# One down unit earlier, first transfers reordered, an idle bank and a scalar-engine transpose in a two-block transformer kernel

## The reference

```python
# first block, per layer: 8 + 2 heads, an index branch, a convolution branch, a recurrence, a gated FFN
xn = rms_norm(h, norm_mix[l]); proj = xn @ w_in[l]            # 1024 x 7464
y_a = dsa_attention(rope(q), rope(k), v, rope(qi), rope(ki), wi)   # top-64 keys of each query by an index score
y_b = sc_b * causal_dwconv(sc_c * sc_u, w_conv)
y_c = rwkv7_time_mix(rw_z, ...)   # state = state*w + (state @ ka)*kb + v*k over 256 steps, 8 heads
up = einsum('bsgc,gcd->bsgd', [y_a, y_b, y_c], w_branch[l])
h = h + sum(sigmoid(gate_pre + b_gate) * up) @ w_out[l]
h = h + (silu(conv(x @ w_up)[gate]) * conv(x @ w_up)[up]) @ w_down      # d_ff = 2816
# second block, per layer
u = rms_norm_2(x, norm_w) @ w_in                               # 1024 x 10240
ya = dilated_mixture(rope(qa), rope(ka), va) * silu(za)
ob = diff_attention(..., lam)     # lam = exp(lq1.lk1) - exp(lq2.lk2) + lambda_init
x = x + (sigmoid(ga) * (ya @ w_proj_a) + sigmoid(gb) * (yb @ w_proj_b)) @ w_out
```

## Time and profile before

| | us |
|---|---|
| median of 3 runs (lowest, highest) | 1663.52 (1663.13, 1664.37) |
| the profiled execution: its own time | 1662.3 |
| the profiled execution: its span | 1660.5 |
| PE busy | 1639.6 (99%) |
| DVE busy | 1186.5 (71%) |
| ACT busy | 970.8 (58%) |
| POOL busy | 191.3 (12%) |
| mean granted TensorE clock | 0.997 of full speed |

### The profile page before, as it was taken

The page is one execution under the profiler, slowest core; times in us unless marked ns, Lnnn a source line. Parts: engine busy times, 40 slices in busy tenths (PEclk is TensorE's granted clock), DMA queues, the critical chain, the costliest instruction groups (busy, mean ns, idle before and its releaser), DMA issues.

```text
span 1660.5 us, 27388 instructions
## 1 busy us (share of the span) xinstructions
PE 1639.6 (99%) x11188; PEld 1418.6 (85%) x11188; DVE 1186.5 (71%) x1666; ACT 970.8 (58%) x1484; POOL 191.3 (12%) x197
## 2 busy tenths in 40 slices
PE   8999999999999999999999999999999999999998
PEld 6999999988888999998988877778888887787886
DVE  6877456699888976547798885767756657667655
ACT  6674525565567565345655565665774546657743
POOL 0673500000001845200000000000000000000000
PEclk9999999999999999999999999999999999999999
DMA  7543532555555534425455555345345464344452
GB/s 268 174 153 109 178 116 103 180 177 202 179 194 182 173 106 140 160 103 178 152 200 199 178 186 194 131 149 174 130 162 188 170 204 151 130 175 144 141 197 76
DMA packets 48621, 270.11 MB, mean 163 GB/s; under 512 B 13617, under 2 KB 14513, under 8 KB 16753
## 3 DMA queue, kind: packets, MB, share of 16 engines
q1 hardware_dynamic: 38304, 265.22, 46.1%
q10 hardware_dynamic: 9424, 2.10, 0.6%
q0 software_dynamic: 768, 1.05, 0.2%
HBM read 266.51 MB, written 1.84 MB: 162 GB/s over the span
## 4 chain that ended last, share of the span: by engine, by line
PE 87%; DVE 7%; ACT 3%; issue 1%; DMA 1%; DVEq 0%; SPq 0%; ACTq 0%
PE bank L2769 10%; PE bank L2771 10%; PE bank L2770 10%; PE bank L1569 8%; PE bank L1570 7%; PE bank L1571 7%; PE bank L1627 7%; PE bank L1629 3%; PE bank L1730 3%; PE bank L1732 3%; PE bank L1731 3%; DVE w_low L1017 3%; DVE arena L1202 2%; PE bank L2799 2%; ACT w_high L605 1%
## 5 line engine op out<-in xcount | busy, mean ns | idle before, releaser
L1017 DVE TENSOR_TENSOR w_low<-slab,w_high 128x2048 fp32r<-128x2048 f32 x249 | 574.3, 2316 | 206.8 <-ACT w_high L605 199.7
L605 ACT ACTIVATE w_high<-slab 128x2048 fp32r<-128x2048 f32 x249 | 470.5, 1897 | 118.2 <-PE bank L2771 70.0
L1569 PE MATMUL bank<-act,w_high 128*128 128x256 f32 (+1 forms) x1136 | 328.7, 289 | 1.5 <-DVE w_low L1017 1.0
L1570 PE MATMUL bank<-act,w_high 128*128 128x256 f32 (+1 forms) x1136 | 321.2, 283 | 0.0
L1571 PE MATMUL bank<-act,w_low 128*128 128x256 f32 (+1 forms) x1136 | 321.1, 283 | 0.0
L2769 PE MATMUL bank<-w_high,act 128*128 128x512 f32 x768 | 305.6, 398 | 0.8 <-DVE act L2536 0.6
L2771 PE MATMUL bank<-w_low,act 128*128 128x512 f32 x768 | 299.8, 390 | 0.0
L2770 PE MATMUL bank<-w_high,act 128*128 128x512 f32 x768 | 299.0, 389 | 0.0
L1569 PEld LDWEIGHTS bank<-act,w_high 128*128 128x128 f32 (+1 forms) x1136 | 216.3, 190 | 10.8 <-issue 5.6
L1570 PEld LDWEIGHTS bank<-act,w_high 128*128 128x128 f32 (+1 forms) x1136 | 216.5, 191 | 0.7 <-issue 0.5
L1571 PEld LDWEIGHTS bank<-act,w_low 128*128 128x128 f32 (+1 forms) x1136 | 216.4, 190 | 0.0
(11 more groups left out here) (272 smaller groups left out, 2131.6 us busy)
## 6 DMA issues: line engine op xcount, KB each, us to landing
slab<-stream_a SPq DMA_DIRECT2D x143, 1024.0 KB, 4.9
slab<-stream_b SPq DMA_DIRECT2D x104, 1024.0 KB, 4.9
arena<-x_t SPq DMA_DIRECT2D x4, 256.0 KB, 6.7
slab<-stream_a ACTq DMA_DIRECT2D x2, 512.0 KB, 6.1
residual<-x_tok SPq DMA_DIRECT2D x1, 1024.0 KB, 10.9
lora_weights<-lora SPq DMA_DIRECT2D x2, 512.0 KB, 9.2
lora_weights<-final_rows SPq DMA_DIRECT2D x2, 512.0 KB, 5.8
d_inverse<-arena POOLq DMA_DIRECT2D x2, 256.0 KB, 2.4
```

The source lines that it names most:

```text
L605: line.did(eng.activation(core.wh[u % PARTS][:, 0:SLAB_WIDTH[u]], core.slab[u % SLABS][:, 0:SLAB_WIDTH[u]], ACT.Copy), core.sem("slab_high"))
L1017: line.did(line.eng.tensor_tensor(core.wl[u % PARTS][:, 0:SLAB_WIDTH[u]], core.slab[u % SLABS][:, 0:SLAB_WIDTH[u]], core.wh[u % PARTS][:, ...
L1569: eng.matmul(out, wh, xh, start=first, stop=False, skip_group_check=True)
L1570: eng.matmul(out, wh, xl, start=False, stop=False, skip_group_check=True)
```

## The change

Down unit i stands behind up unit 2i+4 instead of 2i+5 (except the last three, which stay at the end). The first transfers go x, slab 1, slab 2, tokens, 128 KB of the constants, slab 3; `vec_a`, the rest of the constants, slab 4, `const_a`, `lora` and slab 5 follow. The sines are computed ahead of everything else on ACT, with their table as the first one loaded; the root table is loaded before slab 1 is rounded, and squares, norm and rotary tables of stage a0 come behind unit `w0`. `post(1)` uses bank 5 instead of 7. POOL no longer makes the transposed copy nor writes to DRAM: ACT does both (`flip`, ahead of `gb0`), and the sixteen read-backs are shared, eight by ACT (ahead of `gb2`), eight by POOL. The split of the last quarter of the mixture stands behind the split of the next slab (`mix_low`). In the second block the product behind `lam` is made at the start of a stage, `norm` stands behind `v` unit 0, and the two extra squares of b0 behind its transposes. Semaphores that are merged (`rates_made`, `lora_inputs`, `model_in`) keep their meaning; those hunks, the table of counts and the hunks that only pass new names are left out here.

```diff
@@ -47,18 +47,15 @@
            + [("out", i) for i in range(4)])
-LAG_DOWN = 2
 NARROW_UP = 4
 def ffn_units():
-    units = []
-    for pair in range(FT // 2 + LAG_DOWN):
-        if pair < FT // 2:
-            units += [("up", 2 * pair), ("up", 2 * pair + 1)]
-        if pair >= LAG_DOWN:
-            units.append(("down", pair - LAG_DOWN))
-    return units
+    downs = FT // 2
+    units = [("up", j) for j in range(3)]
+    for i in range(downs - 3):
+        units += [("up", 2 * i + 3), ("up", 2 * i + 4), ("down", i)]
+    return units + [("up", FT - 3), ("up", FT - 2), ("up", FT - 1)] + [("down", i) for i in range(downs - 3, downs)]
 UNITS_A += ffn_units()
@@ -241,6 +238,7 @@
 GEMM_BANKS = 3
+ATTENDED = (6, 5)
 def plan(units):
@@ -358,11 +356,10 @@
     if first:
-        steps = [("angles", 0)]
+        steps = [("angles", 0), ("angles", 1)]
         for n in range(2):
             steps += [("scaled", n), ("round_half", n), ("split_half", n)]
-        return (steps + [("scaled", 2), ("scaled", 3), ("round", 1), ("split", 1), ("angles", 1), ("root_table", 0),
-                         ("square", 0), ("square", 1), ("angles", 2), ("norm", 0)])
+        return steps + [("scaled", 2), ("scaled", 3), ("root_table", 0), ("round", 1), ("split", 1)]
     return [("add", 0), ("add", 1), ("add", 2), ("scaled", 0), ("scaled", 1), ("add", 3), ("square", 0), ("square", 1), ("split", 1)]
@@ -421,6 +418,8 @@
         amid(("w", 0), ("x_turn", 2), ("x_turn", 3))
+    if first:
+        put(("w", 0), ("square", 0), ("square", 1), ("norm", 0), ("angles", 2))
     amid(("w", 1), *([] if first else [("norm", 0)]), ("tables", 0))
@@ -447,8 +446,9 @@
     put(("ga", 3), ("tok", 2))
+    amid(("gb", 0), ("flip", 0))
     put(("gb", 0), ("off_diag", 0), ("bonus_shift", 0))
-    put(("gb", 2), ("blocks_in", 0))
+    amid(("gb", 2), ("blocks_in", 0))
     put(("gb", 3), ("solve", 0))
@@ -460,6 +460,7 @@
     amid(("br2", 1), ("mix", 0))
+    put(("br2", 1), ("mix_low", 0))
     amid(("out", 2), ("x_ffn", 0), ("x_ffn", 1))
@@ -490,8 +491,10 @@
                 put(UNITS_B[host + n], ("turn_late", 8 * kind))
-    mid = {("v", 0): [("x_turn", 2), ("x_turn", 3)], ("v", 1): [("norm", 0)]}
+    mid = {("v", 0): [("x_turn", 2), ("x_turn", 3)]}
+    put(("v", 0), ("norm", 0))
     if first:
+        mid["v", 0] += [("square", 2), ("square", 3)]
         mid["out", 3] = [("x_next", 0), ("x_next", 1)]
@@ -510,9 +513,7 @@
     put(("out", 2), ("root_table", 0))
-    lead = lead_steps(False)
-    if first:
-        lead[lead.index(("split", 1)):] = [("square", 2), ("square", 3), ("split", 1)]
+    lead = [("lam_product", 0)] + lead_steps(False)
     return woven(UNITS_B, False, lead, after, mid, not first, behind_mid=[("v", 0)])
@@ -550,22 +551,25 @@
     slab_to(core, eng, 1)
+    slab_to(core, eng, 2)
     eng.dma_start(core.h[:], d["x_tok"]).then_inc(sem("tokens_in").sem, 16)
-    eng.dma_start(core.cc[:], d["common"]).then_inc(sem("const_in").sem, 16)
-    slab_to(core, eng, 2)
-    eng.dma_start(core.cm[:], d["const_a"]).then_inc(sem("model_in").sem, 16)
-    eng.dma_start(core.vec[:], d["vec_a"][0]).then_inc(sem("vec_in").sem, 16)
-    eng.dma_start(core.lora[:], d["lora"][0]).then_inc(sem("lora_in").sem, 16)
+    eng.dma_start(core.cc[:, 0:2 * P], d["common"][:, 0:2 * P]).then_inc(sem("const_in").sem, 16)
     for u in range(SLABS, SLABS_IN_ALL):
...
         slab_to(core, eng, u)
+        if u == SLABS:
+            eng.dma_start(core.vec[:], d["vec_a"][0]).then_inc(sem("vec_in").sem, 16)
+            eng.dma_start(core.cc[:, 2 * P:], d["common"][:, 2 * P:]).then_inc(sem("model_in").sem, 16)
+        if u == SLABS + 1:
+            eng.dma_start(core.cm[:], d["const_a"]).then_inc(sem("model_in").sem, 16)
+            eng.dma_start(core.lora[:], d["lora"][0]).then_inc(sem("lora_in").sem, 16)
         if u == FIRST_SLAB["a1"] + SLABS:
...
         if u == FIRST_SLAB["b0"] - 20:
-            eng.dma_start(core.cb[:], d["const_b"]).then_inc(sem("const_b_in").sem, 16)
+            eng.dma_start(core.cb[:], d["const_b"]).then_inc(sem("model_in").sem, 16)
             eng.wait_ge(sem("g_made").sem, START["b0"]["g_made"])
@@ -655,6 +659,18 @@
              core.sem("rooted_sums"))
+def inverses_from(core, eng, by, blocks):
+    eng.wait_ge(*core.sem("inverses_written").next(eng, 16))
+    for at, turned, name in ((TD_, 1, "transposes_in"), (UD_, 0, "inverses_in")):
+        to = flat(core, at, 4).rearrange("p (cj t) -> p cj t", cj=16)
+        for n in blocks:
+            q = n % 4
+            eng.dma_start(to[SUB * n:SUB * n + SUB, :, SUB * q:SUB * q + SUB],
+                          core.d_inverse[SUB * n:SUB * n + SUB, turned, :].rearrange("cj (i t) -> i cj t", i=SUB)
+                          ).then_inc(core.sem(f"{name}_{by}").sem, 16)
 WIDTH = {0: P, 1: T}
@@ -863,7 +879,7 @@
         eng.wait_ge(*sem("outputs_turned").next(eng))
-        act(core.xh[:, 2 * n:2 * n + 2, :], heads(bank[6 + n], T), ACT.Copy, sem("ya_high"))
+        act(core.xh[:, 2 * n:2 * n + 2, :], heads(bank[ATTENDED[n]], T), ACT.Copy, sem("ya_high"))
     def lora_inputs(_):
@@ -929,15 +945,18 @@
                 sem("blocks_written").sem, 16)
+    def flip(_):
+        both = flat(core, UT_, 2)
+        eng.wait_ge(*sem("inverted").next(eng))
+        ut = both.rearrange("p (w i t) -> p w i t", w=2, i=SUB)
+        act(ut[:, 1], ut[:, 0].rearrange("p i t -> p t i"), ACT.Copy)
+        line.settled()
+        eng.dma_start(core.d_inverse, both.rearrange("p (w n) -> p w n", w=2)).then_inc(sem("inverses_written").sem, 16)
     def blocks_in(_):
-        eng.wait_ge(*sem("inverses_written").next(eng, 16))
-        to = flat(core, UD_, 4).rearrange("p (cj t) -> p cj t", cj=16)
-        for n in range(8):
-            q = n % 4
-            eng.dma_start(to[SUB * n:SUB * n + SUB, :, SUB * q:SUB * q + SUB],
-                          core.d_inverse[SUB * n:SUB * n + SUB, 0, :].rearrange("cj (i t) -> i cj t", i=SUB)
-                          ).then_inc(sem("inverses_in").sem, 16)
+        inverses_from(core, eng, "act", range(4, 8))
     def solve(s):
@@ -986,7 +1006,7 @@
     eng.wait_ge(*sem("eps_set").next(eng))
-    line.did(eng.activation(core.small[:, 6:7], core.small[:, 0:1], ACT.Copy))
+    line.did(eng.activation(core.small[:, 6:7], core.small[:, 0:1], ACT.Sin))
     eng.wait_ge(sem("gains_in").sem, 16)
@@ -1258,7 +1278,7 @@
                     did(tt(flat(core, GA_ + at, 2), flat(core, GA_ + at, 2), src, ALU.add), sem("summed"))
-                if g == 2 and (i or k):
+                if g == 2 and i + k == 1:
                     for at_ in ((0, 2) if i == 0 else (at,)):
@@ -1271,6 +1291,9 @@
             ffn(i)
+    def mix_low(_):
+        low(14, 2, core.a(GA_ + 6, 2), "mix_high", "mix_ready")
     def ki_turn(_):
@@ -2011,7 +2037,7 @@
             eng.wait_ge(sem("dve_emptied7").sem, banks.count[7, "dve"])
-        b = 6 + n
+        b = ATTENDED[n]
         banks.fill(b, "dve")
@@ -2290,13 +2318,7 @@
     def blocks_in(_):
-        eng.wait_ge(*sem("inverses_written").next(eng, 16))
-        to = flat(core, TD_, 4).rearrange("p (cj t) -> p cj t", cj=16)
-        for n in range(8):
-            q = n % 4
-            eng.dma_start(to[SUB * n:SUB * n + SUB, :, SUB * q:SUB * q + SUB],
-                          core.d_inverse[SUB * n:SUB * n + SUB, 1, :].rearrange("cj (i t) -> i cj t", i=SUB)
-                          ).then_inc(sem("transposes_in").sem, 16)
+        inverses_from(core, eng, "pool", range(4))
     def blocks_turn(_):
@@ -2321,11 +2343,7 @@
             did(tt(above, above, term, ALU.add))
-        line.settled()
-        did(eng.tensor_copy(ut[:, 1], u.rearrange("p i t -> p t i")))
-        line.settled()
-        eng.dma_start(core.d_inverse, flat(core, UT_, 2).rearrange("p (w n) -> p w n", w=2)).then_inc(
-            sem("inverses_written").sem, 16)
+        line.tell(sem("inverted"))
     def off_diag(_):
@@ -2554,17 +2573,18 @@
         if stage == "b0":
-            eng.wait_ge(sem("const_b_in").sem, 16)
+            eng.wait_ge(sem("model_in").sem, 48)
         line.settled()
...
         line.settled()
-    def lam(_):
+    def lam_product(_):
         q = core.gains[:, GN["lam"] + 4 * layer:][:, 0:4].rearrange("p (n two) -> p n two", two=2)
         did(tt(core.small[:, 14:16].unsqueeze(2), q[:, :, 0:1], q[:, :, 1:2], ALU.mult), sem("lam_products"))
+    def lam(_):
         eng.wait_ge(*sem("act_emptied6").upto(1))
```

More of the change, by code:

```diff
@@ L874, in lora @@
             for b in range(2):
-                eng.wait_ge(*sem(("decay_made", "rate_made")[half]).next(eng))
+                eng.wait_ge(*sem("rates_made").upto(2 * b + half + 1))
                 for k in range(2):
@@ L978, in scalar_a @@
                                scores=scores, turn=turn, post=post, lora_inputs=lora_inputs, lora=lora, decay=decay, blend=blend,
-                               kk_square=kk_square, kk_root=kk_root, tok=tok, blocks_out=blocks_out, blocks_in=blocks_in, solve=solve,
```

(11 more changed lines are left out.)

37 lines of the change are left out of this document (21 added, 16 removed).

## The result

The changed kernel takes **1652.80 us** (median of 6 runs, 1652.70 to 1653.18), the one before 1663.14 on the same chip (6 runs, 1661.46 to 1664.37): ratio 0.9937, 95% interval 0.9927 to 0.9947. The forecast was 1653.5, with a range of 1649.5 to 1658.0. The profiled execution took 1652.78 with a span of 1651.0: 9.5 us less than before, where the sum said 9.9. By the medians the gain is 10.3: the kernel before spreads over 2.9 us and the changed one over 0.5. In the runs of the kernel before that stand beside the experiments, those with a mean granted clock of 0.999 or 1.0 took 1661.15 to 1662.98 and those with 0.997 took 1662.65 to 1664.50; every run of the changed kernel had 0.999 or 1.0.

What follows compares the result with a forecast made beforehand. PE, busy 1639.6 of 1660.5 us, was taken as the bound, leaving idle time and half-clock stretches to win. Terms of 9.9 us off 1662.3 gave 1652.4; 1.2 for the median made 1653.5, range 1649.5 to 1658.0.

Steps and rivals of the forecast that it cites:

- the sum: All six parts together: 3.6 + 2.4 + 0 + 1.0 + 1.0 + 1.9 = 9.9 us gained.
- Part 1: Start: slab 3 rounded earlier, q0 at full clock, a new wait at `turns`; gain 3.6 us, bounds 2.5 and 6.
- The table load: ACT at the start: a load costs 1.28 us without the skill's 1.38 drain, which would cut the gain by about 1.4.
- Part 2: Bank 5 for `post(1)`: PE's two waits for ACT's copy out of bank 7 go, 2.4 us in the sum.
- Part 3: Inverses shared between ACT and POOL: worth 0 us, bounds -1 and +1, as it protects the gain of bank 5.
- PE shows no wait at the solve steps now: Solve steps: no wait listed now, and none expected after the bank and inverse changes, hence 0 us.
- Its side: ACT's `flip`: at 179.3 less the start's gain; slab `gb3` keeps some 6 us to spare, so PE doesn't see it.
- Rival D: ACT stands in `flip`, delaying the rounding for `gb3` past its 6 us to spare: slower, 1667.6 us; chance 0.03.
- Part 4: `mix_low` behind the split: the wait in front of the second output unit goes, 0.48 each, 1.0 us.
- Part 5: Down units earlier: front gains 1.1 to 1.3, last down unit loses 0.8; 0.5 a layer, 1.0 us.
- Part 6: Second block: the wait for `lam` goes, 1.86 with restart; moving norm and squares gives and takes 0.6; net 1.85 us.

Runs made afterwards that it cites:

- act_old: The changed kernel with the scalar and vector engines' steps of the start in the old order, transfers in the new order: 1654.40 us, ratio to before 0.9947.
- dma_old: The changed kernel with the first transfers in the old order, everything else as changed: 1655.69 us, ratio to before 0.9955.
- ffn_old: The changed kernel with the old order of up and down units in both layers: 1653.30 us, ratio to before 0.9940.
- flip_old: The changed kernel with bank 5 kept but the inverses made the old way (POOL copies and writes): 1655.64 us, ratio to before 0.9956.
- flip_bank_old: The changed kernel with the inverses made the old way and the second pair of attention outputs in bank 7: 1656.36 us, ratio to before 0.9962.
- bank7: The changed kernel with the second pair of attention outputs turned into bank 7 again, all else as changed: 1655.51 us, ratio to before 0.9953.

## Why the prediction was right, and where its steps were not

- **Part 1**, 3.6 forecast, 3.45 measured, by its own steps: tokens at 16.09 (16.0), slab 3's rounding at 19.00 (18.9), q0 at 24.81 behind a wait of 0.92 (24.7, 1.2), `turns` at 38.19 (38.1). The clock stayed at 2.4 GHz through waits of 0.9 and 1.75 us, and of 1.7 in act_old; it was at 1.2 behind the one of 3.07 in dma_old and the one of 2.93 in the kernel before. The 3.6 held 2.8 for DVE's chain and 0.8 for the slowed PE that trailed behind it; measured are 2.70 and 0.75. In dma_old the slow clock cost nothing, as it lay beneath DVE's chain, and it was low for less long: the granted clock of 27 to 33 and of 33 to 41 us is 0.72 and 1.00 there, 0.50 and 0.97 in the kernel before.
- **The table load**: 1.28 us, and the next activation 0.02 later, again. The 1.38 us of drain that the Trainium skill (ScalarE: Activation LUTs, What ACT_TABLE_LOAD costs) adds would, by an estimate from that figure, have put slab 1's rounding at 14.3 and not at 12.94. The measurement decides.
- **Part 2**, 2.4 forecast, 2.60 measured.
- **Part 3**: nothing in the sum, and 0.04 in the table. The prediction did say that part 3 protects part 2, but bounded it at one us, and it is worth 2.7 once bank 5 is in. The step that failed is "PE shows no wait at the solve steps now": no wait of PE in the list is no margin (0.04 us were to spare), and part 2 had just brought PE 1.3 us nearer. The sum came out because both parts were made together. Nor did the protection come the way it was forecast. POOL's read-backs were to begin 1.6 earlier than before, at 186.6; they began at 183.72, which with PE 4.75 earlier is 0.2 later against PE than before, since POOL waited 1.0 for the write. What gave PE room is that two engines share them, the transposed ones first: these had landed at 191.90, 1.0 us ahead of PE.
- **Its side**, `flip`: forecast at 179.3 less the start's gain, 175.9, it came at 178.35 (ACT's timeline):

```profile
178.35 0.66 ACT L710 ACTIVATE arena<-arena 128x256 f32<-128x256 f32 x1 [3.40 <-POOLq L138]
179.04 0.34 ACTq L955 DMA_DIRECT2D d_inverse<-arena  x1
```

  ACT stood 3.4 us. The 2.45 by which it was late are for the most part a split of DVE's that bank 5 brought into POOL's inversion (last section). The spare time at unit gb3 fell from 5.25 to 2.18. Rival D's mechanism was at work, with 2 us left before it would have cost.
- **Part 4**, 1.0 forecast, 1.24 in the table and 1.25 by undoing it.
- **Part 5**, 1.0 forecast, 0.1 measured. The front gave 1.16 and 1.08, as forecast, and the waits of 0.1 and 0.3 that were to be left there did not come. The tail took 1.03 and 1.24 and not 0.8. The start of the last down unit is 0.7 of it, where 0.8 was forecast. The unit before it starts 0.15 late, and not for a split (its own ended 2.4 us earlier) but for the low half of its hidden tile, which DVE finished at 478.64, 0.15 ahead of PE. Another 0.17 and 0.37 are lost between the start of the last down unit and the next stage; against ffn_old, 0.13 of it stands in the unit's first products behind the wait, and in the second layer 0.16 more at the transposes (L1784, 0.8 instead of 0.6). The term that was mis-sized is the tail, where only the split for the last down unit was counted.
- **Part 6**, 1.85 forecast, 2.14 measured: the wait for lambda was 2.03 with what it stalls, not 1.86.

The sum of 9.9 against 9.5 owes something to chance: part 5 was 0.9 too high, parts 2, 4 and 6 together 0.7 too low. So does the 1653.5: it added 1.2 us for a median above the profiled execution, which the kernel before showed, and the changed kernel shows 0.02. That error and the 0.4 of the sum pull opposite ways, and 0.7 is left.

## What to carry to other kernels

A wait that is not in the list is not a margin. Before an engine is brought forward, look up when each of its later inputs is ready, above all transfers, and not just which of them it waits for now: bank 5 alone would have kept 1.0 of its 2.6 us (flip_old against flip_bank_old). When work is moved earlier in an order written by hand, the cover that one end wins is paid for at another: put the payment where the slack is widest. Moving the three ups from the end to the middle turned 0.1 us into 2.3. And where two engines slow each other when they meet, as DVE and POOL do here, moving one of them changes what the other one's work takes.

## What the runs showed of the hardware that was not expected

**POOL stands while DVE splits a slab.** A step of the inversion that takes 0.24 to 0.31 us takes 2.2 to 2.4 where it meets a split. Timeline of POOL and of DVE, in the kernel before, then in the changed one, then of DVE and ACT in bank7:

```profile
172.15 2.25 POOL L2323 TENSOR_TENSOR arena<-arena 128x64 f32<-128x64 f32 x1
...
171.90 2.32 DVE L1017 TENSOR_TENSOR w_low<-slab,w_high 128x2048 fp32r<-128x2048 f32 x1 [0.76 <-ACT w_high L605]
179.72 2.40 DVE L1017 TENSOR_TENSOR w_low<-slab,w_high 128x2048 fp32r<-128x2048 f32 x1 [5.50 <-ACT w_high L605]
```

```profile
168.48 2.43 POOL L2343 TENSOR_TENSOR arena<-arena 128x64 f32<-128x64 f32 x1
...
175.04 2.33 POOL L2343 TENSOR_TENSOR arena<-arena 128x28 f32<-128x28 f32 x1
...
168.45 2.29 DVE L1037 TENSOR_TENSOR w_low<-slab,w_high 128x2048 fp32r<-128x2048 f32 x1 [0.76 <-ACT w_high L609]
174.98 2.29 DVE L1037 TENSOR_TENSOR w_low<-slab,w_high 128x2048 fp32r<-128x2048 f32 x1 [4.24 <-ACT w_high L609]
```

```profile
176.35 2.29 DVE L1037 TENSOR_TENSOR w_low<-slab,w_high 128x2048 fp32r<-128x2048 f32 x1 [5.54 <-ACT w_high L609]
...
176.33 0.67 ACT L710 ACTIVATE arena<-arena 128x256 f32<-128x256 f32 x1
```

In the 14 traces, both layers, 52 splits fall within POOL's inversion (with its copy, where it has one), and exactly 52 steps there take 2.2 to 2.8 us: each overlaps one split, and the inversion's steps end 0.1 to 0.2 us behind it. A step that has already begun when the split begins keeps its 0.24 to 0.31. In flip_bank_old the split meets the copy (2.80 instead of 0.63); in the kernel before later splits meet the products behind the inversion (3.94 instead of 1.90 at 184.35), and there DVE pays too (a split of 3.39 at 183.15). What the two engines share is not shown by any run here.

The kernel before has one split within the inversion; the next began at 179.72, just behind it. The changed kernel has two, 2.1 us more on the chain that `flip` waits for, which is most of its 2.5 us of delay against the forecast. bank7 tells why: POOL's program is the same there, but PE waits for bank 7 and the splits come 1.4 us later, the inversion has one split again, and `flip` starts at 176.33, 2.0 us sooner than in the changed kernel.

**The same write of 256 KB lands after 2.0 to 5.3 us**: 2.0 in bank7 and 2.4 in the kernel before, where no slab was under way when it was issued, 3.6 in flip_old's second layer, where a slab of 1 MB was issued 2.0 us ahead of it, 4.4 in the changed kernel (1.7 ahead) and 5.3 in flip_bank_old (0.8 ahead). Bringing PE forward brings the slabs' transfers forward too, and here onto the write.
